# A state-space prologue in which loads, zeroing and output tables change place

## The reference, cut to what matters

```python
def s5_mixer(u, lam_re, lam_im, log_dt, b_re, b_im, c_re, c_im, d_skip, w_glu):
    lam = lax.complex(lam_re, lam_im)
    dt = jnp.exp(log_dt)[:, None]
    a_bar = jnp.exp(lam * dt)                                        # 64 groups x 64 states
    b_bar = ((a_bar - 1.0) / lam)[..., None] * lax.complex(b_re, b_im)
    bu = jnp.einsum('blgh,gph->blgp', ug, b_bar)                     # ug: 64 groups of 16 channels
    _, states = lax.associative_scan(_ssm_combine, (a_seq, bu), axis=1)
    y = jnp.einsum('blgp,ghp->blgh', states, c).real.reshape(bsz, length, D_MODEL)
    y = y + d_skip * u
    y = jax.nn.gelu(y)
    val, gate = jnp.split(y @ w_glu, 2, axis=-1)
    return val * jax.nn.sigmoid(gate)
```

## Time and profile before

| | |
|---|---|
| Median of three runs | 1945.39 us (1945.06 to 1946.08) |
| The profiled execution itself | 1944.47 us |
| Its span in the trace | 1942.4 us |
| Mean granted clock of TensorE | 0.992 |
| PE / DVE / ACT / POOL busy over the span | 97% / 40% / 42% / 44% |
| PE busy from 0 to 60 us | 41.7 us |

### The profile page before, as it was taken

The page is one execution under the profiler, slowest core; times in us unless marked ns, Lnnn a source line. Parts: engine busy times, 40 slices in busy tenths (PEclk is TensorE's granted clock), DMA queues, the critical chain, the costliest instruction groups (busy, mean ns, idle before and its releaser), DMA issues.

```text
span 1942.4 us, 26536 instructions
## 1 busy us (share of the span) xinstructions
PE 1890.6 (97%) x9610; PEld 1528.6 (79%) x9610; DVE 774.6 (40%) x1382; ACT 807.5 (42%) x1179; POOL 856.8 (44%) x421
## 2 busy tenths in 40 slices
PE   6999999999999999999999999999998999999997
PEld 4878788888887786578888888877885888888886
DVE  7852232222016999825222200456477062222103
ACT  4663344443125444835344421446246254344211
POOL 6544354444433243844444444434335444444441
PEclk9999999999999999999999999999999999999998
DMA  2143242333232232022323232332320323323331
GB/s 107 27 148 98 74 127 87 98 96 99 96 97 87 66 98 76 1 67 89 105 86 105 90 103 95 101 98 76 131 76 1 98 90 94 104 90 98 98 97 44
DMA packets 51832, 170.81 MB, mean 88 GB/s; under 512 B 6696, under 2 KB 11560, under 8 KB 51248
## 3 DMA queue, kind: packets, MB, share of 16 engines
q1 hardware_dynamic: 50320, 164.99, 27.4%
q10 hardware_dynamic: 1440, 4.83, 0.7%
HBM read 165.34 MB, written 2.10 MB: 86 GB/s over the span
## 4 chain that ended last, share of the span: by engine, by line
PE 91%; DVE 5%; ACT 1%; DMA 1%; DVEq 1%; issue 1%; SPq 0%; ACTq 0%
PE ps L238 24%; PE ps L240 24%; PE ps L239 24%; PE ps L1590 3%; PE ps L1592 3%; PE ps L1591 3%; PE ps L1289 2%; PE ps L1303 1%; PE ps L1311 1%; PE ps L820 1%; DVE h_lo L1212 1%; DVE xT L1135 1%; DMA s_gains<-in_s_gain 1%; PE ps L1629 1%; PE ps L1609 0%
## 5 line engine op out<-in xcount | busy, mean ns | idle before, releaser
L228 POOL TENSOR_TENSOR w_lo<-raw,w_hi 128x1024 fp32r<-128x1024 f32 x296 | 712.8, 2417 | 972.9 <-ACT w_hi L221 972.9
L238 PE MATMUL ps<-h_hi,w_hi 128*128 128x512 f32 (+1 forms) x1456 | 570.6, 392 | 4.2 <-DVE h_lo L1212 2.8
L240 PE MATMUL ps<-h_hi,w_lo 128*128 128x512 f32 (+1 forms) x1456 | 566.8, 389 | 0.0
L239 PE MATMUL ps<-h_lo,w_hi 128*128 128x512 f32 (+1 forms) x1456 | 566.6, 389 | 0.0
L221 ACT ACTIVATE w_hi<-raw 128x1024 fp32r<-128x1024 f32 x296 | 311.5, 1057 | 487.5 <-PE ps L240 436.8
L238 PEld LDWEIGHTS ps<-h_hi,w_hi 128*128 128x128 f32 (+1 forms) x1456 | 272.2, 187 | 64.5 <-issue 7.5
L240 PEld LDWEIGHTS ps<-h_hi,w_lo 128*128 128x128 f32 (+1 forms) x1456 | 272.1, 187 | 58.3
L239 PEld LDWEIGHTS ps<-h_lo,w_hi 128*128 128x128 f32 (+1 forms) x1456 | 272.3, 187 | 57.7 <-issue 0.5
L238 PE MATMUL ps<-hid_hi,w_hi 128*128 (+1 forms) x528 | 205.4, 389 | 0.0
L239 PE MATMUL ps<-hid_lo,w_hi 128*128 (+1 forms) x528 | 205.4, 389 | 0.0
L240 PE MATMUL ps<-hid_hi,w_lo 128*128 (+1 forms) x528 | 205.4, 389 | 0.0
(11 more groups left out here) (379 smaller groups left out, 2096.2 us busy)
## 6 DMA issues: line engine op xcount, KB each, us to landing
raw<-in_w_gu SPq DMA_DIRECT2D x132, 512.0 KB, 3.5
raw<-in_w_down SPq DMA_DIRECT2D x66, 512.0 KB, 3.5
raw<-in_w_mix SPq DMA_DIRECT2D x33, 512.0 KB, 3.5
raw<-in_w_dsa SPq DMA_DIRECT2D x29, 512.0 KB, 3.5
raw<-in_w_glu SPq DMA_DIRECT2D x16, 512.0 KB, 3.8
raw<-in_w_out SPq DMA_DIRECT2D x12, 512.0 KB, 3.5
raw<-in_w_o SPq DMA_DIRECT2D x8, 512.0 KB, 3.5
s_x<-in_xs SPq DMA_DIRECT2D x1, 2048.0 KB, 11.2
```

The lines of the kernel that those rows point to most:

```text
L228: pool.tensor_tensor(w_lo[slot][:], raw[slot][:], w_hi[slot][:].bitcast(F32), ALU.subtract)\
L238: pe.matmul(o, wh, ah, start=start, stop=False)
L239: pe.matmul(o, wh, al, start=False, stop=False)
L240: return pe.matmul(o, wl, ah, start=False, stop=stop)
```

## The change

In seven parts:

- **Loads.** SP starts `dskip`, then the first quarter of `braw` and of `gains` (what steps 0 and 1 need), then the first half of the input. After the parameters have landed it starts the second half of the input, and after `dskip` has landed `chunks` and `craw`. ScalarE starts the other three quarters of `braw` and `gains` later, after its first sine and square, and not before the first quarters have landed.
- **Powers.** VectorE forms the fraction of the angle before it waits for the constants, and forms `wave` after it.
- **Zeroing.** `toep` is zeroed by VectorE instead of GpSimd.
- **Skip matrix.** GpSimd forms `dI` for 16 groups in the prologue, and for 8 more in `begin` and in each of steps 1 to 5.
- **Order on ScalarE.** In `begin` the copies of the matrices come before the angles. The square root moves into a function with a wait for the constants ahead of its old wait.
- **Order on GpSimd.** The first `states_out` waits until the second `winT` is formed.
- **Identity products.** Twelve instead of six: five ahead of the sums, two behind them, two behind the matrices of step 0, three in the place of the six.

```diff
 def s5_sync(sp):
             sp.dma_start(vec[:], d["vec"]).then_inc(consts_landed, 16)
-            sp.dma_start(xs[:], d["xs5"]).then_inc(S["x_landed"], 16)
+            sp.dma_start(dskip[0:GH, :], d["s5_d"]).then_inc(S["cx_landed"], 16)
+            sp.dma_start(braw[:, :, FIRST_TWO], d["s5_b"][:, :, FIRST_TWO]).then_inc(S["bc_landed"], 16)
+            sp.dma_start(gains[:, FIRST_TWO], d["s5_gain"][:, FIRST_TWO]).then_inc(S["bc_landed"], 16)
+            sp.dma_start(xs[:, 0:G // 2, :], d["xs5"][:, 0:G // 2, :]).then_inc(S["x_landed"], 16)
+            sp.wait_ge(S["par_landed"], 16)
+            sp.dma_start(xs[:, G // 2:G, :], d["xs5"][:, G // 2:G, :]).then_inc(S["par_landed"], 16)
+            sp.wait_ge(S["cx_landed"], 16)
             sp.dma_start(chunks[0:2 * QP, :, :], d["s5_chunks"]).then_inc(S["cx_landed"], 16)
             sp.dma_start(craw[:], d["s5_c"]).then_inc(S["cx_landed"], 16)
-            sp.dma_start(dskip[0:GH, :], d["s5_d"]).then_inc(S["cx_landed"], 16)
 def s5_gpsimd(pool):
+            pool.memset(c_pair[:], 0.0)
             for p in range(2):
-                pool.memset(toep[p][:], 0.0)
                 pool.memset(decay[p][:], 0.0)
-            pool.memset(c_pair[:], 0.0)
-            pool.drain().then_inc(S["zeroed"], 2)
+            pool.drain().then_inc(S["zeroed"], 1)
...
+            def skips(g0, g1):
+                pool.tensor_tensor(dI[0:GH, g0:g1, :], bc(dskip[0:GH, g0:g1], 2, GH), bc(ident[0:GH, 0:GH], 1, g1 - g0), ALU.mult)
 begin (gpsimd)
                 angles(e, p)
-                skips()
+                pool.wait_ge(S["par_landed"], 16)
+                pool.wait_ge(S["cx_landed"], 16)
+                pool.tensor_tensor(dskip[0:GH, :], dskip[0:GH, :], gain5[0:GH, :], ALU.mult)
+                pool.drain()
+                skips(0, 2 * QG)
                 pool.wait_ge(S["ang_reduced"], 1)
                 angles(e + 1, 1 - p)
                 pool.wait_ge(S["prologue"], 1)
                 inputs(e)
                 weigh(e + 2)
+                skips((e + 2) * QG, (e + 3) * QG)
                 inputs(e + 1)
+                pool.wait_ge(S["winT_ready"], e + 2)
                 states_out(e, p)
 s5_scalar
-            act.wait_ge(consts_landed, 32)
-            act.dma_start(braw[:], d["s5_b"]).then_inc(S["bc_landed"], 16)
-            act.dma_start(gains[:], d["s5_gain"]).then_inc(S["bc_landed"], 16)
...
-            act.wait_ge(S["x_landed"], 16)
+            act.wait_ge(S["bc_landed"], 16 * 2)
+            act.dma_start(braw[:, :, OTHERS], d["s5_b"][:, :, OTHERS]).then_inc(S["bc_landed"], 16)
+            act.dma_start(gains[:, OTHERS], d["s5_gain"][:, OTHERS]).then_inc(S["bc_landed"], 16)
             for g in range(0, G, QG):
+                act.wait_ge(*((S["x_landed"], 16) if g < G // 2 else (S["par_landed"], 32)))
...
-            act.wait_ge(S["sumsq"], 1)
-            act.activation(rstd5[:], sumsq[:], ACT.Sqrt, bias=eps, scale=1.0 / D).then_inc(S["std"], 1)
+            def token_roots():
+                act.wait_ge(consts_landed, 32)
+                act.wait_ge(S["sumsq"], 1)
+                act.activation(rstd5[:], sumsq[:], ACT.Sqrt, bias=eps, scale=1.0 / D).then_inc(S["std"], 1)
 begin (scalar)
+                token_roots()
+                matrices_out(e, p, use)
                 angles(e, p)
-                matrices_out(e, p, use)
 s5_vector
+            for p in range(2):
+                dve.memset(toep[p][:], 0.0)
+            dve.drain().then_inc(S["zeroed"], 1)
...
-            dve.wait_ge(consts_landed, 32)
             dve.tensor_scalar(f1, phi, 1.0 / (2 * math.pi), None, ALU.mult)
...
+            dve.wait_ge(consts_landed, 32)
             dve.tensor_tensor(wave[:], bc(rho, 1, CH + 1), tau, ALU.mult).then_inc(S["turn"], 1)
...
             dve.tensor_tensor(turn[:], bc(f1, 1, CH + 1), tau, ALU.mult)
 s5_tensor
+            def warm(bank, times):
+                for _ in range(times):
+                    pe.matmul(ps[:, bank, :], ident, cst[:, 0:T], start=True, stop=True)
+
+            warm(Y_BANK, 5)
             for n in range(NQ):
...
+            warm(Y_BANK, 2)
             pe.wait_ge(S["std"], 1)
 begin (tensor)
                 matrices(e)
+                warm(Y_BANK, 2)
                 inputs(e, p)
                 transposed_ratio()
-                for _ in range(6):
-                    pe.matmul(ps[:, PT_BANK[0], :], ident, cst[:, 0:T], start=True, stop=True)
+                warm(PT_BANK[0], 3)
                 matrices(e + 1)
```

More of the change, by code:

```diff
@@ L321, in s5_steps @@
             last(NQ - 1, 1, NQ // 2)
+        FIRST_TWO, OTHERS = slice(0, 2 * QG * GH), slice(2 * QG * GH, G * GH)
         def s5_sync(sp):
@@ L394, in states_out @@
                 pool.drain().then_inc(S["wout_ready"], 1)
[L396 to L402, removed]
+            def skips(g0, g1):
+                pool.tensor_tensor(dI[0:GH, g0:g1, :], bc(dskip[0:GH, g0:g1], 2, GH), bc(ident[0:GH, 0:GH], 1, g1 - g0), ALU.mult)
             def weigh(e):
                 cols = slice(e * QG * GH, (e + 1) * QG * GH)
-                pool.wait_ge(S["bc_landed"], 16 * 2)
+                pool.wait_ge(S["bc_landed"], 16 * 4)
                 pool.tensor_tensor(braw[:, :, cols], braw[:, :, cols], bc(gains[:, cols], 1, 2), ALU.mult)
@@ L557, in s5_vector @@
             dve.drain()
-            dve.wait_ge(consts_landed, 32)
             tau = bc(const("tau"), 2, GP)
             dve.tensor_scalar(f1, phi, 1.0 / (2 * math.pi), None, ALU.mult)
-            dve.tensor_tensor(wave[:], bc(rho, 1, CH + 1), tau, ALU.mult).then_inc(S["turn"], 1)
             dve.drain()
@@ L571, in s5_vector @@
             dve.drain()
+            dve.wait_ge(consts_landed, 32)
+            dve.tensor_tensor(wave[:], bc(rho, 1, CH + 1), tau, ALU.mult).then_inc(S["turn"], 1)
             dve.tensor_tensor(turn[:], bc(f1, 1, CH + 1), tau, ALU.mult)
```

## The result

The changed kernel takes 1951.61 us (median of seven runs, 1950.53 to 1952.75); the kernel before, beside it, 1945.15 (1944.08 to 1946.80). The ratio is 1.0034, 95% interval 1.0024 to 1.0043: slower by more than the 0.2% that can be told here, and outside the predicted range of 1937.3 to 1943.0. The profiled execution took 1950.53, its span is 1948.7, the mean granted clock 0.988 (before 0.992).

A forecast was written before the change was run, and what follows sets the result against it. The bound was taken to be a chain of waits through all engines up to line 820. 4.8 + 0.7 + 0.3 - 0.2 = 5.6 us earlier, so a median of 1939.8 us, range 1937.3 to 1943.0.

The forecast's parts named there:

- the one on the skip matrix: GpSimd's skip matrix in pieces: first `winT` product 1.23 us earlier; six pieces of 0.35 cost 0 to 0.2 a step.
- Contention does not go, it moves: Rival, chance 0.22: pieces hit the additions, second and third `winT` stay as long, step 3 costs 0.8; gain 2.9, 1942.5 us.
- the slower rival: TensorE stays at half clock, identity products are paid in full: 1953 us; chance 0.10, half slower, half about no change.
- Powers and zeroing: VectorE's start: first product by 3.1, two clears of 1.9 us done at 2.7, tables ready 0.93 earlier, weighing at 15.35.
- First `winT` product alone: VectorE's first `winT` product, with no GpSimd work beside it, takes 1.22 us instead of 2.45: 1.23 earlier.
- Input in halves: First half squared from 9.8, ten identity records fill 4.9 to 11.8, TensorE's sums end at 18.7 instead of 23.84.
- Square root: ScalarE's table load ahead of the square root is no longer hidden and comes onto the chain: 1.33 us later.
- Copies before angles: ScalarE copies first, so VectorE adds the skip at 26.1 instead of 30.19; the order gives 2.4 us of that.
- `states_out` behind the second `winT`: Less GpSimd work beside VectorE's second `winT`: 0.7 us saved (bounds 0 to 1.1), ready at 32.4.
- Line 842 of step 0: Line 820 before the change: starts at 38.9 instead of 43.70, 4.8 us earlier, from 1.67 + 2.4 + 0.7.
- Step 1: Third `winT` 0.7 us shorter, TensorE's clock gives 0.3; line 820 of step 1 near 52.2 instead of 57.77.
- A second term: GpSimd, some 3 us behind, touches VectorE's products for step 3: a loss of 0.2 us.

The follow-up runs named there:

- the kernel with breaks: The changed kernel with a GpSimd drain ahead of each of the four products of `states_out`: 1949.11 us, ratio 1.0019.
- The kernels with 64 and 16 partitions: Changed kernel, whole skip matrix in the prologue, in each piece's place a GpSimd product of constants over 64 or 16 partitions: 1955.35 and 1953.21 us.

## Why the prediction was wrong

**The step that failed** is the one on the skip matrix: "The six pieces of 0.35 go into GpSimd's free time of over 4 us a step; bounds 0 to 0.2 a step". Alone a piece lasts near what was said (0.39); beside a VectorE product it lasts 1.38 (45.63). The free time it counted on isn't there in steps 0 and 1: in the kernel before GpSimd runs from 27.73 to 56.05 with no pause but its drains' 0.18, and only then stands idle, for 5.5. And I asked only what else waits while a piece runs, not what becomes of GpSimd's instructions behind it. The pieces bring two waits, 4.95 for an addition that took 1.23 in the kernel before, and 6.74 for a product that took 2.13. Shown in both directions: without the pieces the changed kernel is 7.5 us faster; put alone into the kernel before, they cost 8.5. None of the rivals was this one. "Contention does not go, it moves" named the pieces hitting the additions, but priced them by the rows of before; and the slower rival, TensorE at half clock in the sums, didn't happen: the 16 records of the sums took 7.13 us, 0.45 each, against 9.70.

The earlier steps, one by one:

- *Powers and zeroing*: VectorE's first product started at 3.40, not by 3.1. Two clears of 0.91 were 1.9 as estimated, but began at 1.29, not 0.7. The late start was named as a sign of being wrong, and cost little here: weighing came at 15.71 for 15.35.
- *First `winT` product alone*: 1.22 for 1.22, right. The skip matrix for 16 groups, charged with 0.2 ahead of the weighing, lay beside one small step of VectorE's (0.50); the whole matrix in its place makes the weighing 1.3 later.
- *Input in halves*: the first half is squared from 11.36, not 9.8, inside its bounds; the sums end at 19.17 for 18.7. TensorE idled 1.42 ahead of them, another sign named as wrong, since its ten identity records took 6.16 and not 6.9, and the first half of the input came late; its clock stayed up all the same.
- *Square root*: the exposed table load came as forecast (22.50 to 23.78), and moving one wait hides it again, for 1.2 us of line 842.
- *Copies before angles*: right; the skip was added at 26.41 for 26.1, but took 1.32 beside the scaling and not 0.87.
- *`states_out` behind the second `winT`*: here the 0.7 failed. From its start at 28.25 the second `winT` took 5.43, against 5.61 before: the second product took 2.15 beside GpSimd's scaling, and `winT` was there at 33.68 for 32.4. The best version does without this wait.
- *Line 842 of step 0*: 42.22 for 38.9. Of the 3.3, 1.3 are the second `winT`. 2.05 are the clock: the kernel with breaks, whose instructions from 12 to 33.7 start within 0.2 us of this one's, kept its clock, and started line 842 at 40.17. The forecast counted on the clock staying up between the second `winT` and line 842, and had no row for a fall behind an idle of 1.61 us. These 2.05 do not reach the end: the chain goes from `zout` at 39.36 into VectorE's wait, not through line 842.
- *Step 1*: 63.95 for 52.2. Here the two long waits stand.

**A second term was too small**, and the pieces hide it. With the skip matrix whole and all else as in the change, the kernel is 1.3 us under the one before, which can't be told from no change, and not 5.6. In its profile line 842 starts 2.6 earlier than before for step 0, 4.05 earlier for step 1, and only 1.3 earlier for step 2 (68.29 for 69.62). Between the last two its timeline has these rows:

```profile
55.62 1.41 DVE L679 TENSOR_TENSOR s_winT<-s_table,s_b 128x1024 f32<-128x1024 f32 x1
...
57.11 2.13 DVE L684 TENSOR_TENSOR s_wtmp<-s_table,s_b 128x1024 f32<-128x1024 f32 x1
...
59.32 1.98 DVE L689 TENSOR_TENSOR s_winT<-s_winT,s_wtmp 128x1024 f32<-128x1024 f32 x1
...
61.35 0.66 PE L791 MATMUL ps<-cst,s_winT 128*128 128x128 f32 x4 [1.15 <-DVE s_winT L689]
```

GpSimd's `states_out` now lies beside the products for step 3, which took 1.22 to 1.23 each before, and TensorE's clock is at 0.50 from 63.5 to 66.5. The interval is 14.57, where before it was 11.85. The forecast had 0.2 for this ("GpSimd, some 3 us behind, touches step 3's products"), and the rival "Contention does not go, it moves" 0.8. The forecast also took a shift of line 820 for a shift of the end, which doesn't hold at step 1. In the fastest kernel the interval is 12.95. Its 4.0 us (1941.34) are for more than the change without its pieces: the table load is freed, the wait left out, and 48 groups of the skip matrix are in one later product.

## What to carry to other kernels

Before a short GpSimd instruction is put into a row of long ones, look at what stands behind it up to the next drain, and at what VectorE needs in that time: in these kernels a product over 16, 32 or 64 partitions at its head made VectorE wait for the whole row. A drain behind it, or a place at the row's end, cured that. When a wait is moved, see on which instruction the compiler puts it, since a table load with a wait doesn't hide.

## What the hardware did that I had not expected

- A GpSimd product over 16, 32 or 64 partitions ahead of a row of five 128x512 products keeps VectorE's products with two SBUF inputs waiting until the row pauses: 4.95 to 6.75 us in six kernels. Over 128 partitions, at the same time and length, 0.72 to 2.14. Why the width decides isn't known; widths between 64 and 128 weren't tried.
- TensorE's clock falls in one execution and stays in another behind the same rows. From 12 us on the changed kernel and the one with breaks agree to within 0.2 us up to 33.7, with the same idle of 1.61 us; then the clock is at 0.50 from 35 to near 42 in the first and at 1.00 in the second, and line 842 of step 0 starts at 42.22 and 40.17. So the fall costs 2.05 us at that line. The kernels with 64 and 16 partitions differ as much there (43.55 and 41.49), but the second had its clock down at 26 to 28 as well; and by step 1, behind VectorE's long waits, they are level (66.55 and 66.46). Why it falls in one and not in the other isn't known.
